# Second-block attention of a two-block transformer: keys on rows, split operands and a block of ones, and modulation tiles moved beside the MLPs

## The reference, cut to what matters

```python
q_nope, q_rope = (rms_norm(p[:, :384]) @ w_uq)      # 64 + 32 numbers a head; the 32 are rotated for x
k_nope, v      = (rms_norm(p[:, 384:640]) @ w_ukv)  # 64 and 64 numbers a head
s    = q_nope . k_nope + q_rope . k_rope            # k_rope: 32 numbers, one set for all heads
prob = softmax(s / sqrt(96), over keys)             # x: 768 keys (x and context); context: its own 256
out  = prob @ v
```

## Time and profile before

| | |
|---|---|
| median of three runs | 2711.88 us (2703.31 to 2712.36) |
| profiled execution, its own time | 2711.97 us |
| its span (first to last instruction) | 2710.2 us |
| mean granted clock of PE | 0.94 of full speed |
| PE busy | 2458.2 us, 91% of the span |
| DVE, ACT, POOL busy | 1340.7, 901.3, 593.1 us |
| DMA queues of SP, of POOL | 165.04 MB and 62.95 MB, 19.4% and 7.7% of 16 engines |

### The profile page before, as it was taken

How to read it: one execution, slowest core, us unless ns; L and a number is a source line. 1 busy time by engine, 2 the same in 40 slices (tenths; PEclk the granted TensorE clock), 3 DMA queues, 4 the chain that set the end, 5 groups by cost and what they waited for, 6 DMA issues and landing times.

```text
span 2710.2 us, 28175 instructions
## 1 busy us (share of the span) xinstructions
PE 2458.2 (91%) x10858; PEld 1831.0 (68%) x10858; DVE 1340.7 (49%) x2023; ACT 901.3 (33%) x1459; POOL 593.1 (22%) x519
## 2 busy tenths in 40 slices
PE   5899846999999799789889999999899898999998
PEld 4664315777788587444578888888767445788886
DVE  4775554478765644643443333333463644443434
ACT  5124533332223421245433222222142454432222
POOL 1320022232332121200113221222031201222221
PEclk9998766899999899999889999999999999899999
DMA  5761100256665122100112221221132111233331
GB/s 175 239 199 31 39 0 27 93 193 192 211 217 159 34 96 68 53 18 24 33 45 70 62 65 61 63 70 55 51 97 76 33 32 47 76 95 94 95 92 55
DMA packets 70113, 232.94 MB, mean 86 GB/s; under 512 B 8095, under 2 KB 11280, under 8 KB 69980
## 3 DMA queue, kind: packets, MB, share of 16 engines
q1 hardware_dynamic: 49328, 165.04, 19.4%
q0 software_dynamic: 17600, 62.95, 7.7%
q10 hardware_dynamic: 3052, 3.13, 0.4%
HBM read 223.20 MB, written 7.90 MB: 85 GB/s over the span
## 4 chain that ended last, share of the span: by engine, by line
PE 74%; DVE 11%; ACT 5%; issue 4%; POOL 3%; DMA 2%; ACTq 0%; DVEq 0%; POOLq 0%
PE psum L503 34%; PE psum L736 20%; PE psum L1064 4%; PE psum L1035 3%; DVE mod_scratch_b L1211 2%; PE psum L992 2%; PE psum L560 2%; PE psum L637 1%; DVE mod_scratch_a L1211 1%; DMA mod_ring_a<-in_w_mod 1%; PE psum L1050 1%; POOL weight_split L2518 1%; PE psum L474 1%; PE psum L461 1%; PE psum L665 1%
## 5 line engine op out<-in xcount | busy, mean ns | idle before, releaser
L503 PE MATMUL psum<-mix_split,weight_split 128*128 128x512 f32 (+1 forms) x3840 | 801.7, 370 | 25.0 <-DVE mix_split L1450 12.8
L503 PEld LDWEIGHTS psum<-mix_split,weight_split 128*128 128x128 f32 x3840 | 662.4, 190 | 165.9 <-issue 27.6
L736 PE MATMUL psum<-hidden,weight_split 128*128 128x512 f32 (+1 forms) x3072 | 633.9, 366 | 5.5 <-POOL weight_split L2518 2.8
L736 PEld LDWEIGHTS psum<-hidden,weight_split 128*128 128x128 f32 x3072 | 523.4, 188 | 112.7 <-POOL weight_split L2518 4.7
L1940 ACT CAST weight_split<-weight_ring 128x1024 fp32r<-128x1024 f32 x269 | 276.4, 1041 | 308.5 <-PE psum L736 295.6
L2518 POOL TENSOR_TENSOR weight_split<-weight_ring,weight_split 128x1024 fp32r<-128x1024 f32 x89 | 233.8, 2627 | 495.8 <-ACT weight_split L1940 494.9
L1479 DVE TENSOR_TENSOR hidden<-hidden_tmp,hidden 128x512 fp32r<-128x512 f32 (+1 forms) x128 | 136.6, 1087 | 394.9 <-POOL hidden_tmp L2667 394.9
L1127 DVE TENSOR_TENSOR weight_split<-weight_ring,weight_split 128x1024 fp32r<-128x1024 f32 x180 | 231.8, 1290 | 27.7 <-ACT weight_split L1940 27.6
L2215 ACT ACTIVATE hidden_tmp<-psum 128x512 f32<-128x512 f32 (+1 forms) x128 | 69.2, 540 | 526.1 <-PE psum L503 526.1
L1496 DVE SCALAR_TENSOR_TENSOR residual<-psum,modulation,residual 128x512 f32<-128x512 f32 x192 | 120.7, 657 | 214.0 <-PE psum L736 214.0
L503 PE MATMUL psum<-normed_in,weight_split 128*128 128x512 f32 (+1 forms) x1080 | 217.0, 361 | 9.6 <-DVE normed_in L1181 6.9
(11 more groups left out here) (286 smaller groups left out, 2371.3 us busy)
## 6 DMA issues: line engine op xcount, KB each, us to landing
weight_ring<-in_w_mlp SPq DMA_DIRECT2D x128, 512.0 KB, 3.6
mod_ring_b<-in_w_mod POOLq DMA_DIRECT2D x68, 512.0 KB, 4.0
weight_ring<-in_w_ff SPq DMA_DIRECT2D x64, 512.0 KB, 4.3
weight_ring<-in_w_in SPq DMA_DIRECT2D x45, 512.0 KB, 4.3
mod_ring_a<-in_w_mod POOLq DMA_DIRECT2D x28, 512.0 KB, 4.6
weight_ring<-in_w_out SPq DMA_DIRECT2D x24, 512.0 KB, 3.6
weight_ring<-in_tables SPq DMA_DIRECT2D x13, 512.0 KB, 3.6
weight_ring<-in_w_v SPq DMA_DIRECT2D x8, 512.0 KB, 5.2
```

The costliest lines, as they stand in the source:

```text
L503: m = pe.matmul(psum[:, b + r, 0:hi - lo], w[:, part_w, :], x[:, part_x, k, lo:hi], start=k == 0 and part_w + part_x == 0, stop=k == KT - ...
L736: mm = pe.matmul(psum[:, b + r, 0:hi - lo], w[:, part_w, :], G[:, part_x, f % (2 * GROUP), lo:hi], start=jj == 0 and part_w + part_x == 0, ...
```

## The change

**Attention.** One list, `mla_steps(l)`, now sets the order of all four engines. K and Q are split into high and low parts (`k_split`, `q_split`); ACT writes the high part out of PSUM, DVE the low one. For each head:

- `scores`: queries on partitions as before, but of high parts only. They serve DVE for the negated maximum of each row and nothing else.
- `shift`: PE turns the 128 maxima of a query tile into a row of 128 columns (1 x 128, float32), four times for x and twice for the context; ACT copies the row into row 96 of Q's high part. Row 96 of K is one, so the product itself subtracts the maximum.
- `turned`: 128 keys by 512 (or 256) queries, keys on partitions, in three terms of 97, 96 and 96 rows. Steps 0 to 5 are the key tiles for x, 6 and 7 those of the context.
- ACT computes the exponential twice, once as float32 and once as float32r; POOL subtracts (`prob_lo`).
- `values`: three terms, accumulated over the key tiles. The 128 stationary columns are 64 of V and 64 more, all ones in the high part and zero in the low one. So 64 partitions of the result hold the sums and the other 64 hold the denominators, each of them 64 times.
- DVE takes the reciprocal of the 64 x 512 (64 x 256) denominators out of PSUM and multiplies.

There are no transposes of probabilities. Banks: "scores" 0 and 2 (pairs), "turned" 4 and 5, "sum" 6 for the values of x, and "project" 7 for Q, K, shift rows and the context's values. At the start ACT copies V into its high parts, and POOL forms the low ones and fills ones and zeros.

**Modulation.** No tile lies beside the first input projection any more. 64 tiles, all with two vectors, lie beside the first MLP (128 dot products). The 32 tiles of layer 1 that need one vector are fetched in halves of 512 columns beside the MLP of layer 0 (`late_modulation`, 64 dot products of 512 columns).

The core of the diff:

```diff
+        MOD_TILES = [(0, t) for t in range(48)] + [(1, t) for t in range(16)]
+        MOD_LATE = [(t, half) for t in range(16, 48) for half in range(2)]
...
+        def mla_steps(l):
...
+                for j in range(nj):
+                    steps.append(("turned", h, j))
+                    if j < 2 and h % 2 and h + 1 < MH:
+                        steps.append(("k", (h + 1) // 2, j))
+                    if j == 0 and 0 < h < MH - 1:
+                        steps.append(("rope", h + 1, 0))
+                    if j > 1:
+                        steps.append(("values", h, j - 2))
+                        if h + 1 < MH and j - 2 < 4 + ctx:
+                            steps.append(("scores", h + 1, j - 2))
+                for r in range(1 + ctx):
+                    if h + 2 < MH:
+                        steps.append(("q", h + 2, r))
+                    if h + 1 < MH:
+                        steps.append(("shift", h + 1, r))
+                steps += [("values", h, nj - 2), ("values", h, nj - 1)]
+            return steps
...
+            pools = {"turn": [4, 5, 6, 7], "row": [0, 1, 2, 3], "scores": [0, 2], "turned": [4, 5], "sum": [6], "project": [7]}
...
+                def project_q(h, r):
...
+                    freed[b] = [(tag + "_vec", ("q_lo", h, r))]
...
+                def scores(h, i):
...
+                        for a, z in XC:
+                            m = pe.matmul(bank(b, T2, 2)[:, a:z], QS[s][0:96, 0, i * P:(i + 1) * P], KS[l][s][0:96, 0, a:z], start=True, stop=True)
...
+                    freed[b] = freed[b + 1] = [(tag + "_vec", ("max", h, i))]
...
+                def shift(h, r):
...
+                        m = pe.matmul(psum[96:97, b, i * P:(i + 1) * P], mla_st[:, h % 3, 4 * r + i:4 * r + i + 1], C["ident"][:, :],
+                                      start=i == 0, stop=i == n - 1)
...
+                    freed[b] = [(tag + "_act", ("shift", h, r))]
...
+                    if j in (0, 6):
+                        pe.wait_ge(*when(tag + "_act", ("shift", h, j // 6)))
+                        pe.wait_ge(*when(tag + "_vec", ("q_lo", h, j // 6)))
...
+                    for rows, part_k, part_q in ((97, 0, 0), (96, 0, 1), (96, 1, 0)):
+                        m = pe.matmul(psum[:, b, 0:nq], KS[l][s][0:rows, part_k, key:key + P], QS[s][0:rows, part_q, q0:q0 + nq],
...
+                    freed[b] = [(tag + "_act", ("prob_hi", h, j))]
...
+                def values(h, j):
...
+                        b = take(1, "project" if j else "sum")
+                        bank_of[tag, "values", h, j // 6] = b
                         wait_bank(b)
...
-                def logits(n):
...
-                        m = pe.matmul(psum[:, b + off // 512, 0:pw], QH[0:96, h % 3, q:q + P], KH[0:96, h % 3, k0 + off:k0 + off + pw],
-                                      start=True, stop=True)
...
-                def turned(n):
...
-                        for t in range(gn):
-                            m = pe.transpose(psum[:, b, t * P:(t + 1) * P], mla_p[:, n % 3, (g + t) * P:(g + t + 1) * P], C["ident"][:, :])
...
-                def values(u):
...
-                        m = pe.matmul(psum[r0:r0 + DH, b, 0:nq * P], VH[:, k0 // P + t, h * DH:(h + 1) * DH], mla_pt[:, u % 2, t, 0:nq * P],
-                                      start=t == 0, stop=t == w // P - 1)
...
+                    for part_v, prob in ((0, PH[l][n % 4]), (1, PH[l][n % 4]), (0, PL[n % 3])):
+                        if prob is PL[n % 3]:
+                            pe.wait_ge(*when(tag + "_pool", ("prob_lo", h, j)))
+                        m = pe.matmul(psum[:, b, 0:nq], beside_v(part_v, key // P, h), prob[:, 0:nq], start=j in (0, 6) and prob is PH[l][n % 4] and part_v == 0,
...
+                    if j in (5, 7):
+                        freed[b] = [(tag + "_vec", ("mix", h, j // 6))]
...
+                for n, (t, half) in enumerate(MOD_LATE):
...
+                    ve.tensor_tensor_reduce(out=x, in0=x, in1=late_cond[:, 512 * half:512 * half + 512], scale=1.0, scalar=0.0, op0=ALU.mult,
+                                            op1=ALU.add, accum_out=column).then_inc(*did("late_vec", ("dot", n)))
...
+                    for half in range(2):
+                        s = (2 * p + half) % 3
+                        m = ve.tensor_tensor(KS[l][s][0:64, 1, lo:hi], ps[64 * half:64 * half + 64], KS[l][s][0:64, 0, lo:hi].bitcast(F32), ALU.subtract)
+                    m.then_inc(*did(tag + "_vec", ("k_lo", p, r)))
...
+                        ve.tensor_tensor(q_rope[64:96, 0:S], ps[64:96], C["rope"][64:96, :], ALU.mult).then_inc(*did(tag + "_vec", ("q_cos", h)))
+                        ve.tensor_tensor(q_sin, ps[96:128], C["rope"][96:128, :], ALU.mult).then_inc(*did(tag + "_vec", ("q_sin", h)))
+                        ve.wait_ge(*when(tag + "_vec", ("q_sin", h)))
+                        ve.tensor_tensor(q_rope[64:96, 0:S], q_rope[64:96, 0:S], q_sin, ALU.add).then_inc(*did(tag + "_vec", ("q_rope", h)))
+                    ve.wait_ge(*when(tag + "_act", ("q", h, r)))
+                    ve.tensor_tensor(QS[h % 3][0:rows, 1, lo:hi], ps[0:rows], QS[h % 3][0:rows, 0, lo:hi].bitcast(F32),
+                                     ALU.subtract).then_inc(*did(tag + "_vec", ("q_lo", h, r)))
...
+                        m = ve.tensor_reduce(mla_st[:, h % 3, i:i + 1], bank(b, T2, 2), AX.X, ALU.max, negate=True)
...
+                    ve.reciprocal(inverse_sum[r0:r0 + 64, 0:nq], psum[64 - r0:128 - r0, b, 0:nq]).then_inc(*did(tag + "_vec", ("inverse", h, c)))
+                    ve.wait_ge(*when(tag + "_vec", ("inverse", h, c)))
+                    ve.tensor_tensor(H2[r0:r0 + 64, h // 2, q0:q0 + nq], psum[r0:r0 + 64, b, 0:nq], inverse_sum[r0:r0 + 64, 0:nq],
+                                     ALU.mult).then_inc(*did(tag + "_vec", ("mix", h, c)))
...
-                    ac.activation(mla_p[:, n % 3, 0:w], bank(bank_of[tag, "logits", n], w, nb), ACT.Exp, bias=mla_st[:, n % 3, 0:1], scale=1.0,
-                                  accum_out=mla_st[:, n % 3, 1:2]).then_inc(*did(tag + "_act", ("exp", n)))
...
-                    ac.activation(mla_p[:, n % 3, 0:w], mla_p[:, n % 3, 0:w], ACT.Identity, scale=mla_st[:, n % 3, 3:4]).then_inc(*did(tag + "_act", ("prob", n)))
...
+                    ac.activation(PROB[n % 3][:, 0:nq], ps, ACT.Exp).then_inc(*did(tag + "_act", ("prob", h, j)))
+                    ac.activation(PH[l][n % 4][:, 0:nq], ps, ACT.Exp).then_inc(*did(tag + "_act", ("prob_hi", h, j)))
...
+                        ac.copy(v_tile(0, t), VH[:, t, :].rearrange("p (g n v) -> p g n v", n=2, v=V_W)).then_inc(*did(tag + "_act", ("v_hi", t)))
...
+                    po.dma_start(late_ring[:, n % 3, :], dr["w_mod"][1, t][:, 512 * half:512 * half + 512]).then_inc(late_sem[n % 3], 16)
...
-                    next(modulated, None)
                     if i > 2:
                         next(strips_made, None)
-                    if i > 3:
-                        next(modulated, None)
...
+                for part, x in ((0, 1.0), (1, 0.0)):
+                    po.memset(VS[part][:, :, :, 1, :].bitcast(F32), x).then_inc(*did(tag + "_pool", ("beside", part)))
...
+                    po.wait_ge(*when(tag + "_act", ("prob_hi", h, j)))
+                    po.tensor_tensor(PL[n % 3][:, 0:nq], PROB[n % 3][:, 0:nq], PH[l][n % 4][:, 0:nq].bitcast(F32), ALU.subtract).then_inc(*did(tag + "_pool", ("prob_lo", h, j)))
...
-                mlp(f"mlp2_{l}", lambda f: ("w_mlp1", (l, f)), lambda g, m: ("w_mlp2", (l, g, m)), act_tmp_2, RG, iter(()))
+                mlp(f"mlp2_{l}", lambda f: ("w_mlp1", (l, f)), lambda g, m: ("w_mlp2", (l, g, m)), act_tmp_2, RG, iter(()) if l else late_modulation())
```

More of the change, by code:

```diff
@@ L423, in tensor_program @@
         def tensor_program(pe):
-            next_bank = {"pair": 0, "one": 0, "turn": 0, "logits": 0, "row": 0}
-            pools = {"turn": [4, 5, 6, 7], "logits": [0, 2], "row": [0, 1, 2, 3]}
+            next_bank = {"pair": 0, "one": 0, "turn": 0, "row": 0, "scores": 0, "turned": 0, "sum": 0, "project": 0}
+            pools = {"turn": [4, 5, 6, 7], "row": [0, 1, 2, 3], "scores": [0, 2], "turned": [4, 5], "sum": [6], "project": [7]}
             freed = {}
@@ L1508, in beside_mlp @@
             def beside_mlp():
[L1509 removed]
+                yield from modulation()
                 for _ in range(3):
```

730 lines of the change are left out of this document (341 added, 389 removed).

## The result

The changed kernel takes 2808.78 us (median of four, 2805.0 to 2810.56) against 2707.6 us for the kernel before in the same comparison: 1.0373 of it, 95% interval 1.0348 to 1.0398. It is slower by 3.7%, 101 us. The forecast was 2787 us, in a range of 2725 to 2838, 75 us more than before. The profiled execution took 2810.09 us for a span of 2808.3, 98.1 us more than the span before.

The account below looks back on a forecast made before the run. TensorE (PE), busy 91% of the span, was taken as the bound, so only its work or idle time counts. On 2712 us, 47 + 40 (attention) - 24 + 11 + 1 (modulation tiles) = +75 gave 2787 us, range 2725 to 2838.

Parts of the forecast that it names:

- The reciprocal: DVE, attention: 3.85 us for 64x512 and 2.0 for 256 columns, from a slope of 7.2 ns a column.
- The rival that the reciprocal streams: Attention: reciprocal takes 0.68 us like any 512-column operation, long gap 2.0 us, total 2738 us; chance 0.14.
- K: Layer 0 attention: next pair's K waits 2.1 us for the context's reciprocal, its second half 2.2; 4.3 three times.
- The third turned tile: Layer 0 attention: waits 0.9 us for first exponentials, first values 0.4 for GpSimd's low part; 1.3 in 7 heads.
- the sum: Attention stages: work plus waits 238 us in layer 0 and 184 in layer 1; with clock +47 and +40.
- The clock: Both attention stages: pauses lower PE's clock, 3 us for each longer pause, 2 for the others; 18 and 12 us.
- PE's work: Attention: 18.0 us a head, 144 us for layer 0; 14.6 a head, 117 us for layer 1.
- The start: Layer 0 attention: first values some 33 us in, behind POOL's low part of V and ones; 17.5 us lost.
- Modulation tiles: First input projection gets 24 us back (between 12 and 31); first MLP loses 11 us (range 5 to 15).
- The late tiles: Layer 0's MLP: 64 half dots and 64 issues are covered; start activations before two splits cost +1 us.
- GpSimd's subtraction: Attention: 1.29 us, hidden under 1.75 of PE work; rival that GpSimd or DVE bounds, 2815 to 2850 us, chance 0.14.
- Faster: Attention: bank 7 holds cost nothing, total 2659 us; needs gaps under about 30 us in all; chance 0.06.

Follow-up runs that it names:

- e5_banks: Changed kernel with only banks reassigned: one scores pair, Q and K on two banks, shift rows and context values apart, layer 1 values on two; 2687.37 us, ratio 0.9942.
- e8_best: e5_banks plus layer 0's DVE reciprocal after Q's low part, V split earlier, ones and zeros filled earlier, late-vector activations moved later; 2700.83 us, ratio 0.9975.
- e9_best: e5_banks plus late-vector activations six to nine slots into layer 0's MLP, and layer 1's DVE reciprocal one head later; 2683.12 us, ratio 0.9906.

## Why the prediction was right, point by point

- **The mechanism.** PE waits at the shift rows for DVE's low part of Q, twelve times, 4.5 us in layer 0 (5.1 forecast) and 2.9 in layer 1 (3.2 forecast). The other holds of bank 7 in a head were 0.67, 0.91 and 0.46 us for 0.9, 1.15 and 0.7. e5_banks shows that the shared bank is the cause: with its users on banks of their own the two attention stages take 358 us, where they took 478 in the changed kernel and 372 before.
- **The reciprocal.** 3.36 us for 512 columns and 1.76 for 256, for 3.85 and 2.0: 1.60 us for 256 columns more, so 6.25 ns a column. The slope read from 1 to 6 columns was 15% high. The Trainium skill ("VectorE: DVE Perf Modes", the part on the fixed hardware budget) states a repeat count of 8; as an estimate, with the clock of 0.96 GHz that the same page lists, this is 8.3 ns a column and 4.4 us. The measurement is 24% under that, and it decides. The rival that the reciprocal streams is out.
- **K.** Its second half was to wait 2.2 us and its first 2.1; it was 1.4 to 1.5 and 1.1 (chain above: reciprocal ends 1237.37, K starts 1237.96). The third turned tile was to wait 1.3 us in seven heads; the exponentials held PE for 2.2 us in all. So PE's idle time in layer 0 was 72 us and not the 94 of the sum (47 + 2 + 13 + 9 + 17.5 + 6).
- **The clock: a mis-sized term.** "I take 3 us for each of the first, 2 for the others: 18 and 12." The comparison with e5_banks, same matmuls, gives 39.5 us of busy time in layer 0 and 17.0 in layer 1 (150.1 to 133.1). The term was taken from a single pause of 3.4 us after a stretch of full work. In the new stage a second, third and fourth pause follow within 10 us, and the level stays low through Q, shift rows and K: 0.75 of the clock as a mean, where 0.80 to 0.85 was named as the sign. Nor does one pause have one price. Two shift rows in layer 1 of the changed kernel, after the same pause:

```profile
2246.85 1.87 PE L1074 MATMUL psum<-c_ident,mla_max 128*1 128x128 f32 x8 [2.94 <-DVE q_split L1887]
2291.87 1.03 PE L1074 MATMUL psum<-c_ident,mla_max 128*1 128x128 f32 x8 [2.94 <-DVE q_split L1887]
```

The first ran at the lower level, the second at the full one. What decides between them was not tested.
- **The sum, and some luck.** For layer 0 the sum had 144 us of work, 94 of idle time and 18 of clock, 256 in all; the stage took 162.8, 72.0 and 39.5, together 274.3. The idle time was 22 us too high and the clock term 22 too low, which cancelled; what is left is PE's work, 19 us too low. In layer 1 the sum had 117, 67 and 12; measured were 133.1, 54.0 and 17.0. (The 162.8 and 133.1 us are from e5_banks and hold some clock themselves.) So +60.8 for +47 and +45.3 for +40: the range holds the total, but the sizes inside it are less good than the total looks.
- **PE's work.** The sum took 144 us at full clock. The 688 matmuls of layer 0 are busy for 162.8 us at a clock of 0.94 (e5_banks), by busy time times clock 153 us of work at full clock. So, as an estimate, 10 of the 19 us are clock and 9 are work that the pitch does not hold. Which products these are was not measured, nor how the 11.5 us that e5_banks took beyond its 182 divide between this and the start.
- **The start.** 33 us were forecast until the first values, bound by POOL's low part of V. In the changed kernel they come 1144.3 - 1099.9 = 44.5 us in (first line: PE, from the chain), but POOL is done with V and with the ones and zeros at 1135.8 (POOL, from the timeline):

```profile
1144.33 1.28 PE psum L1112 x3
1125.29 7.84 POOL L2785 TENSOR_TENSOR v_lo<-v_heads,v_hi 128x512 fp32r<-128x512 f32 x6 [16.52 <-ACT v_hi L2472]
1134.38 1.38 POOL L2787 MEMSET v_lo<- 128x1536 f32 x1
```

V is there 8.6 us early. The chain of K, Q, scores, maxima and shift rows ends last. That step named the wrong cause; that its 17.5 us of idle time are near the 15.3 us measured there is luck. With the banks apart (e5_banks) the first values come 35.6 us in, and e8_best shows that moving V forward changes nothing then either.
- **Modulation tiles.** -24.7 us for -24 in the first projection and +12.1 for +11 in the first MLP. The late tiles were to cost 1 us and cost 6. The changed kernel's timeline of ACT shows why (in brackets the idle time before):

```profile
1484.56 0.63 ACT L2009 ACTIVATE shifted<-late_cond 128x512 f32<-128x512 f32 x1 [4.21 <-DMA late_cond<-in_cond]
1485.20 1.28 ACT L2011 ACT_TABLE_LOAD   x1
1486.50 0.63 ACT L2011 ACTIVATE shifted<-shifted 128x512 f32<-128x512 f32 x1
1487.15 1.28 ACT L2013 ACT_TABLE_LOAD   x1
```

These steps hold ACT for 15 us in all: 4.2 us of waiting for a fetch that was issued just ahead, six activations, and a table load of 1.28 us ahead of five of them. PE runs out of split weights. The tiles themselves cost next to nothing: with this block moved a few slots on (e9_best) the first products take 70.2 us for 69.3 before.
- **Rivals.** GpSimd's subtraction took 1.30 us for 1.29, and PE waited 0.3 us for it in layer 0; DVE was busy 313 of 434 us in the first MLP and did not saturate. "Faster" failed by the condition set for it: 30 us of gaps in all; the waits for Q's low part alone were 50.

## What to carry to other kernels

Where a list of steps replaces hand-spread work, look at who holds the bank of each step and for how long: a bank that passes from user to user through two other engines turns their delays into PE's pauses, in every turn. Cost the pauses twice, as idle time and as clock; in layer 0 here the clock was as much as the idle time, where several pauses stood close together. Give banks to steps by the time they are held, take them from a use that is soon over (giving up the second pair for the scores cost 4.5 us by the medians; its two banks, given to others, gained 121), and settle the order of the other engines after that: the same reordering was worth +10 us with one set of banks and -16 with the other.
